# Hybrid trunk with two mixture-of-experts layers: six fixed experts instead of four, five groups of four instead of four, and the shared expert's matmuls and the sort behind the routing stage

## The reference

```python
def _moe_ffn(h, w_router, router_bias, w_gate, w_up, w_down, sh_gate, sh_up, sh_down):
    scores = jax.nn.sigmoid(jnp.einsum('bld,de->ble', h, w_router).astype(f32))
    biased = scores + router_bias.astype(f32)
    # 8 groups of 8 experts; the 4 best groups by the sum of their two best; then the best 8 experts
    ...
    w = SCALE * w / jnp.sum(w, axis=-1, keepdims=True)
    # per token: sum over its 8 experts of gate * (silu(h @ w_gate) * (h @ w_up)) @ w_down
    routed = ...
    shared = (silu(h @ sh_gate) * (h @ sh_up)) @ sh_down
    return routed + shared
```

## Time and profile before

| what | us |
|---|---|
| median of 3 runs | 1682.98 (1682.36 to 1685.25) |
| the profiled execution's time | 1685.91 |
| its span, first to last instruction | 1684.1 |
| TensorE busy in the span | 1516.5 (90%), mean granted clock 0.939 |
| experts' block of layer 0, first `gate_up` to last `gate_up` start | 461.80 to 937.61 |

### The profile page before, as it was taken

How to read it: one execution, slowest core, us unless ns; L and a number is a source line. 1 busy time by engine, 2 the same in 40 slices (tenths; PEclk the granted TensorE clock), 3 DMA queues, 4 the chain that set the end, 5 groups by cost and what they waited for, 6 DMA issues and landing times. The chain is left out here.

```text
span 1684.1 us, 25401 instructions
## 1 busy us (share of the span) xinstructions
PE 1516.5 (90%) x9626; PEld 945.3 (56%) x9626; DVE 712.2 (42%) x1610; ACT 367.8 (22%) x765; POOL 249.8 (15%) x324
## 2 busy tenths in 40 slices
PE   8999988899799989979989867989999799799795
PEld 6788668787545435535534455865555345345344
DVE  3879657432434334424433347042343234234323
ACT  3766453210311111101111120131111111011112
POOL 5789336000000000000000000001000000000000
PEclk9999999699899989989999968999999899899898
DMA  7679270022999999999999290395999999999960
GB/s 265 216 169 264 101 200 3 1 90 72 422 376 424 420 425 424 423 421 423 425 419 425 85 365 3 117 375 233 397 424 423 424 422 424 423 420 425 422 280 25
DMA packets 100774, 509.36 MB, mean 302 GB/s; under 512 B 37012, under 2 KB 42196, under 8 KB 65836
## 3 DMA queue, kind: packets, MB, share of 16 engines
q1 hardware_dynamic: 90540, 478.67, 71.4%
q0 software_dynamic: 10112, 29.05, 4.5%
HBM read 506.82 MB, written 17.10 MB: 311 GB/s over the span
## 5 line engine op out<-in xcount | busy, mean ns | idle before, releaser
L1684 PE MATMUL banks<-experts,e_xgT 128*64 128x512 f32 (+1 forms) x1408 | 313.8, 628 | 36.3 <-issue 36.2
L1684 PEld LDWEIGHTS banks<-experts,e_xgT 128*64 128x64 f32 (+1 forms) x1408 | 107.3, 137 | 211.4 <-issue 211.4
L1697 PE MATMUL banks<-x_sg,e_ys 128*128 128x272 f32 (+1 forms) x896 | 209.0, 386 | 2.7 <-ACT e_ys L1776 1.7
L1820 DVE TENSOR_TENSOR e_ac<-e_sl,banks 128x256 f32<-128x256 f32 x56 | 23.6, 421 | 440.0 <-ACT e_sl L1766 440.0
L1805 DVE TENSOR_TENSOR acc<-acc,banks 128x272 f32<-128x272 f32 (+1 forms) x448 | 189.5, 430 | 11.5 <-PE banks L1697 6.3
L268 PE MATMUL banks<-hT,dense_ring 128*128 128x272 f32 x768 | 186.0, 401 | 8.0 <-DMA dense_ring<-in_w_in 8.0
L1295 POOL DMA_INDIRECT x_xg<-rows_dram,x_idx x56 | 55.6, 993 | 874.6 <-DVE x_idx L1287 838.4
L1697 PEld LDWEIGHTS banks<-x_sg,e_ys 128*128 128x128 f32 x896 | 165.9, 190 | 30.7 <-ACT e_ys L1776 3.4
L268 PEld LDWEIGHTS banks<-hT,dense_ring 128*128 128x128 f32 x768 | 148.2, 194 | 42.4 <-issue 11.7
L1684 PE MATMUL banks<-dense_ring,e_xgT 128*64 128x512 f32 (+1 forms) x320 | 150.7, 626 | 16.0 <-issue 16.0
L1719 PE MATMUL banks<-experts,e_aT 128*64 128x512 f32 (+1 forms) x704 | 153.3, 596 | 2.5 <-DVE acc L1805 2.5
(11 more groups left out here) (421 smaller groups left out, 1947.2 us busy)
## 6 DMA issues: line engine op xcount, KB each, us to landing
experts<-in_moe_gate_up SPq DMA_DIRECT2D x88, 2048.0 KB, 26.7
experts<-in_moe_down SPq DMA_DIRECT2D x88, 1024.0 KB, 26.5
dense_ring<-in_moe_gate_up SPq DMA_DIRECT2D x20, 2048.0 KB, 26.1
e_gate_up<-in_moe_gate_up SPq DMA_DIRECT2D x20, 2048.0 KB, 30.7
dense_ring<-in_moe_down SPq DMA_DIRECT2D x40, 1024.0 KB, 26.5
dense_ring<-in_w_in SPq DMA_DIRECT2D x48, 512.0 KB, 4.8
dense_ring<-in_w_out SPq DMA_DIRECT2D x4, 2048.0 KB, 7.7
dense_ring<-in_s_w_out SPq DMA_DIRECT2D x4, 2048.0 KB, 12.0
```

The lines of the kernel that those rows point to most:

```text
L1684: mm = pe.matmul(gub[e * n:(e + 1) * n, :], xgT[:, i % 2, c, e * n:(e + 1) * n], gate_up_weights(mem, j)[:, c, :], start=(c == 0), stop=(c ...
L1697: pe.matmul(cb[m % 4][:, 0:W], ys[:, m * P:(m + 1) * P], sg[:, i % 4, :], start=True, stop=True).then_inc(cmm, 1)
L1820: dve.tensor_tensor(ac[:], sl[:], gub[:, FF:], ALU.mult).then_inc(mul, 1)
```

## The change

- `FIXED` goes from 4 to 6, and three units (`FIXED_UNITS`) of fixed experts are known before the sort.
- `WIDTHS` becomes three pairs, four times a four and four pairs, and a four and three pairs: 27 units, five of them fours. The 20 smallest experts (16 before) have 32 slots.
- Expert 5 (both halves, slot 5) is loaded behind the shared expert's weights in the routing block, in both layers; its buffer is allocated with `experts`. The gate/up half of expert 4 is loaded in the experts' block, when all four shared halves are computed; its down half, as before, behind `shared_down`. SyncE does not wait for the order until `gate_up(0)` is done.
- The routing block ends with the spread of units 0 and 1, their indices and gathers. `shared_half(0)` now follows all row transposes. Half 1, the spread of keys, in layer 0 half 2, then `turn(0)` and the sort's matmuls stand at the head of TensorE's part of the experts' block; the remaining halves (3 in layer 0; 2 and 3 in layer 1) follow `turn_act(0)`. SiLU, gating and the sort's VectorE steps move there too.
- All normalised chunks now come after the sigmoid on ScalarE (`EARLY_NORM` is gone). `xg` is no longer cleared; the copied rows use `xg` and a part of `acc`, and several small tiles use `acc` and `gsb`.

```diff
-FIXED = 4
+FIXED = 6
+FIXED_UNITS = 3
 AHEAD = 3
-EARLY_NORM = 2
...
-WIDTHS = (2, 2) + 3 * (4, 2, 2, 2, 2, 2, 2) + (4, 2, 2, 2, 2)
+WIDTHS = (2, 2, 2) + 4 * (4, 2, 2, 2, 2) + (4, 2, 2, 2)
...
 def gates_in(act, ex, i, banks, W):
     if i >= 2:
-        act.wait_ge(ex["scatter_ready"], i - 1)
+        act.wait_ge(ex["index_summed"], i - 1)
...
 def place_unit(dve, mem, ex, i, banks, W):
+    dve.wait_ge(ex["scatter_ready"], i + 1)
     if i > 0:
         dve.wait_ge(ex["index_ready"], i)
-    dve.scalar_tensor_tensor(out=ex["hit"][:], in0=banks[0][:, 0:W], scalar=mine, in1=mem["tok"][:, 0:W],
+    dve.scalar_tensor_tensor(out=ex["gsb"][:, i % 2], in0=banks[0][:, 0:W], scalar=mine, in1=mem["tok"][:, 0:W],
...
+def shared_banks(mem):
+    return [mem["bank"][b] for b in (6, 7, 6, 7)]
+
+def shared_half(pe, mem, ex, layer, j):
+    q, m = divmod(j, FC)
+    first = first_token(layer)
+    W, w_gu = T - first, shared_weights(mem)[0]
+    if j == 0:
+        pe.wait_ge(mem["shared_gate_up_ready"], 32 * (layer + 1))
+    elif j >= FC:
+        pe.wait_ge(ex["sh_silu"], m + 1)
+    for c in range(DC):
+        mm = pe.matmul(shared_banks(mem)[j][:, 0:W], w_gu[:, c, q * FF + m * P:q * FF + (m + 1) * P],
+                       mem["hT"][:, c, first:], start=(c == 0), stop=(c == DC - 1))
+    mm.then_inc(ex["sh_gate_up"], 1)
...
@@ norm_and_route, @block.sync
                 load_shared(sp, k, mem, layer)
-                if layer == 0:
-                    load_first_experts(sp, k, mem, 0)
+                load_first_experts(sp, k, mem, layer, range(4) if layer == 0 else ())
+                load_gate_up(sp, k, mem, layer, RING - 1, RING - 1)
+                load_down(sp, k, mem, layer, RING - 1, RING - 1)
...
@@ norm_and_route, @block.gpsimd
-                pool.memset(ex["xg"][:], 0.0).then_inc(ex["xg_zero"], 1)
...
@@ norm_and_route, @block.tensor
-                for i in range(min(4, 2 * NT)):
+                for i in range(2 * NT):
                     turn_rows(i)
-                shared_half(0)
-                for i in range(4, 2 * NT):
-                    turn_rows(i)
+                shared_half(pe, mem, ex, layer, 0)
...
-                shared_half(1, range(0, 3))
                 pe.wait_ge(placed, 2)
                 pe.wait_ge(rows_c, 2 * NT)
                 for i in range(2):
                     spread_unit(pe, mem, ex, i, spread_ps[i], W)
-                shared_half(1, range(3, DC))
-                shared_half(2)
-                pe.wait_ge(keyed, 1)
-                pe.matmul(key_ps[0:E, 0:E], ones[0:E, 0:E], keys[:], start=True, stop=True).then_inc(spread, 1)
-                shared_half(3)
-                pe.wait_ge(placed_by, 2)
-                pe.matmul(sort_ps[:, 2 * E:2 * E + 1], twice, rank[:], start=True, stop=True)
...
@@ experts, @block.sync
-                for j in range(FIXED, RING):
-                    load_gate_up(sp, k, mem, layer, expert(j), j)
-                load_down(sp, k, mem, layer, expert(RING - 1), RING - 1)
                 for i, stream in enumerate(UNITS):
                     after = [j + RING for j in stream if j + RING < E]
                     if after:
                         sp.wait_ge(gu, i + 1)
+                        if i == 0:
+                            sp.wait_ge(ordered, 2)
                         for j in after:
                             load_gate_up(sp, k, mem, layer, expert(j), j)
+                        if i == 0:
+                            sp.wait_ge(sh_gu, 2 * FC)
+                            load_gate_up(sp, k, mem, layer, 4, 4)
                         sp.wait_ge(dn, i + 1)
                         for j in after:
                             load_down(sp, k, mem, layer, expert(j), j)
-                    if i == 0:
-                        sp.wait_ge(sh_dn, DC)
-                        load_down(sp, k, mem, layer, expert(FIXED), FIXED)
+                        if i == 0:
+                            sp.wait_ge(sh_dn, DC)
+                            load_down(sp, k, mem, layer, 4, 4)
...
@@ experts, @block.tensor
+                shared_half(pe, mem, ex, layer, 1)
+                spread_keys()
+                if layer == 0:
+                    shared_half(pe, mem, ex, layer, 2)
                 turn(0)
+                sort_experts()
+                pe.wait_ge(adjusted, 1)
                 broadcast(2)
                 for i in range(len(UNITS)):
                     gate_up(i)
                     if i + 1 < len(UNITS):
                         turn(i + 1)
+                    if i == 0:
+                        pe.wait_ge(ordered, 2)
                     turn_act(i)
+                    if i == 0:
+                        for j in range(2 if layer else 3, 2 * FC):
+                            shared_half(pe, mem, ex, layer, j)
                     if i == 1:
                         shared_down()
...
@@ experts, @block.scalar
+                for m in range(FC):
+                    act.wait_ge(sh_gu, m + 1)
+                    act.activation(shared[:, m, 0:W], shared_banks(mem)[m][:, 0:W], ACT.Silu).then_inc(sh_act, 1)
                 turned_in(0)
```

More of the change, by code:

```diff
@@ L1233, in expert_exchange @@
     sb = lambda name, shape, dt=F32: held.enter_context(nc.sbuf_tensor(f"x{layer}_{name}", shape, dt))
[L1234 to L1237, removed]
+    ex = {"xg": sb("xg", [P, 2, D]), "selw": sb("selw", [P, AHEAD, P]), "gsb": sb("gsb", [P, 2, W]),
+          "sg": sb("sg", [P, 4, W]), "idf": sb("idf", [P, 1]), "idx": sb("idx", [P, 4, 1], I32), "cm": sb("cm", [E, 1])}
+    for name in ("going", "unit_selected", "rows_broadcast", "gates_in", "scatter_ready", "index_summed",
+                 "index_ready", "sh_gate_up", "sh_silu"):
         ex[name] = sem(name)
     ex["gathered"] = [sem("gathered_even"), sem("gathered_odd")]
+    free = mem["acc"][:].rearrange("p c t -> p (c t)")
+    ex["squares"] = mem["acc"][:, :, 0:W]
+    ex["last_rows"], ex["maskT"] = free[:, 0:D], free[0:E, D:D + W]
+    ex["keys"], ex["above"], ex["at_rank"] = (free[0:E, D + T + i * E:D + T + (i + 1) * E] for i in range(3))
     return ex
@@ L1326, in norm_and_route @@
         t8, ws = sb("t8", [P, NT, 8]), sb("ws", [P, NT])
[L1327 to L1335, removed]
+        maskT, cm = ex["maskT"], ex["cm"]
+        loaded = mem["router_loaded"]
         meaned, centred, squared, sq_summed, sd_ready, rooted, scaled, out = (sem(n) for n in (
@@ L1472, in _ @@
                 act.activation(lgT[:], lgT[:], ACT.Sigmoid, bias=bias[:, 0:1]).then_inc(scored, 1)
-                for c in range(EARLY_NORM, DC):
+                for c in range(DC):
                     normal(c)
@@ L1487, in _ @@
                     gates_in(act, ex, i, spread_ps[i], W)
-                for m in range(FC):
-                    act.wait_ge(sh_gu, m + 1)
-                    act.activation(shared[:, m, 0:W], sh_ps[m][:, 0:W], ACT.Silu).then_inc(sh_act, 1)
             @block.vector
@@ L1591, in _ @@
-                link(dve.tensor_tensor(row[:], sort_ps[0:1, E:2 * E], extras[0:1], ALU.add))
-                link(dve.tensor_reduce(rank2[0:1], row[:], AX_X, ALU.max))
-                dve.tensor_copy(mem["count"][:], rank2[0:1]).then_inc(maxed, 1)
 def experts(nc, k, mem, layer, ex):
@@ L1600, in experts @@
     shift, xg, sg = mem["unit_shift"], ex["xg"], ex["sg"]
+    maskT, cm, keys, above, at_rank = (ex[n] for n in ("maskT", "cm", "keys", "above", "at_rank"))
+    sh_gu, sh_act, shared = ex["sh_gate_up"], ex["sh_silu"], mem["shared_act"]
     gate_in, idf_ok, gathered = ex["gates_in"], ex["index_summed"], ex["gathered"]
@@ L1610, in experts @@
         cb = bank[6:] + [y0b, y1b]
-        mem["gate_up_5"] = sb("gate_up_5", [P, GATE_UP])
+        key, rank, extra = (sb(n, [E, 1]) for n in ("key", "rank", "extra"))
+        row, rank2 = sb("row", [1, E]), sb("rank2", [P, 1])
+        sort, key_ps = mem["sort_par"], atb
+        key_off, number, ranks, twice, extras = (sort[:, a:b] for a, b in (
+            (0, 1), (1, 2), (2, 2 + E), (2 + E, 2 + E + P), (2 + E + P, 2 + 2 * E + P)))
+        step, keyed, spread, placed_by, adjusted, sorted_, ordered = (sem(n) for n in (
+            "sort_step", "keys_ready", "keys_spread", "ranks_ready", "places_adjusted", "sorted", "ordered"))
+        sh_mul = sem("sh_gated")
         xgT = sb("xgT", [P, 2, DC, P])
@@ L1824, in _ @@
                         select(i + AHEAD)
+                    if i == 0:
+                        for m in range(FC):
+                            gate(m)
                     if i == 1:
```

125 lines of the change are left out of this document (54 added, 71 removed).

## The result

| | before | after |
|---|---|---|
| median of 20 runs each, us | 1682.34 (1675.95 to 1689.53) | 1692.33 (1685.56 to 1698.61) |
| the profiled execution's time | 1685.91 | 1692.55 |
| its span | 1684.1 | 1689.6 |

The ratio is 1.0055, 95% interval [1.004, 1.007]: the change costs 9.3 us (6.7 to 11.8); the medians lie 10.0 apart, as the ratio is not their quotient. The forecast was 1691.1. The runs of one kernel scatter by more than 10 us, so the ratio carries the verdict, and the spans of two single profiles only locate it.

A forecast was written before the change was run, and what follows sets the result against it. Weight transfers were taken to pace the middle of the experts' stage. Later restarts of +6.4 and +3.1 us, less 1.4 for the tails, gave +8.1: 1682.98 to 1691.1 us; forecast 1688 to 1695 (chance 0.58), range 1681 to 1699.

The forecast's parts named there:

- What bounds the stage: Middle of the experts' stage: weight transfers at 424 GB/s set the pace; a unit less on TensorE only lengthens its waits.
- When the block starts: Experts' block, now begun after GpSimd's second gather: 1.1 us earlier in layer 0, 8 us earlier in layer 1.
- Clock: TensorE at the head of the experts' block: idle beforehand lowers its clock, losing 3.0 us in layer 0, 2.2 in layer 1.
- Restart: SyncE issues expert 4's down half after the last shared_down, then all later experts: 6.4 us later in layer 0, 3.1 in layer 1.
- The hidden part: Early expert loads finish before SyncE's queue resumes behind shared_down; transfers stand still for 4 and 6 us just before.
- Tail: Behind the last four: one unit fewer saves 0.6 to 0.7 us in each layer, 1.4 us for both.
- Sum: Whole kernel: 6.4 + 3.1 - 1.4 = +8.1 us, taking the median from 1682.98 to 1691.1 us.
- 1 (the transfers get the credit): Expert 5's load in layer 1's idle time counts in full, -7.4 us, and -1.4 for the tails: 1674 us; chance 0.10.
- 2 (TensorE): TensorE bounds the experts' stage, so a unit fewer per layer saves 2 by 16.2 us: 1650 us; chance 0.03.
- 3 (no clock loss): TensorE's idle before the experts' block costs no clock, or the block starts earlier: -5.2 us, giving 1686 us; chance 0.17.
- 4 (the gather late behind expert 5): Layer 1's row stores are slowed by expert 5's load, delaying the gather: up to +5 us, giving 1696 us; chance 0.12.
- 5: An expert in a four gets more than its 32 tokens, so extra rounds run; no chance given.

The follow-up runs named there:

- before_widths: The kernel before with only the change's 27 units (five fours) in place of 28: 1680.72 us, ratio 0.9979 to the kernel before.
- after_28units: The changed kernel with 28 units (four fours) as before the change: 1691.52 us, ratio 1.0036 to the kernel before.
- before_reorder: The kernel before with SyncE's wait for shared_down and expert 4's down load moved behind the gate/up loads of experts 8 and 9: 1678.21 us, ratio 0.9969.
- after_fill: The changed kernel with shared halves 1 to 3 and both SiLUs moved back into the routing block behind the spread: 1688.06 us, ratio 1.0007 to the kernel before.
- after_busy: The changed kernel plus dummy matmuls behind the spread (50 in layer 0, 16 in layer 1), which overran the gap: 1702.45 us, ratio 1.012 to the kernel before.
- after_late5: The changed kernel with expert 5's loads issued at the head of the experts' block, not in the routing block: 1688.44 us, ratio 1.0042 to the kernel before.
- after_reorder: The changed kernel with SyncE's wait for shared_down and expert 4's down load behind the gate/up loads of 8 and 9: 1687.42 us, ratio 1.0026 to the kernel before.
- before_both: The kernel before with the change's 27 units and SyncE's shared_down wait behind the gate/up loads of 8 and 9: 1675.62 us, ratio 0.996.

## Why the prediction was right

*What bounds the stage.* Right: 424 GB/s in the middle, waits that grow by what is saved, and an end that follows the restart one to one.

*When the block starts.* Layer 0: forecast 42.5 us after the start of routing, measured 447.86 - 405.4 = 42.5. The gather went out 0.4 us earlier (+39.4), as estimated, but that is within what it does by itself: +39.4 to +39.8 in the four kernels with the order of before's blocks, +39.1 to +39.9 in the eight others. Layer 1: forecast +31.5, measured +35.0. The start follows the second gather by 0.7 us as forecast; the gather itself was 2.9 us later than before. That is no part of the change: it went out between +28.8 and +32.1 in kernels of both kinds (before +29.0, before_widths +32.1, after_28units +29.0). In the profile of after the clock is at 0.50 from 1118.8 to 1125.6, where the stage's sums of squares stand. All twelve profiles fit this: before_widths and before_reorder have such a stretch at the stage's start and gathers at +32.1 and +31.8; after_fill and after_busy have one of 3 to 4 us within the first 6 and gathers at +30.5; the seven others have none there and gathers at +28.8 to +29.1. Why the stretch falls there in some executions stays open. Of these seven, after_late5, after_reorder and after_28units start the block at +31.9 to +32.1, within 0.6 us of the forecast:

```profile
1147.86 6.61 PE L1323 MATMUL banks<-hT,dense_ring 128*128 128x256 f32 x16 [5.13 <-PEq L134]
...
1156.93 7.09 PE L1642 MATMUL banks<-experts,e_xgT 128*64 128x512 f32 x32
```

This is after_late5, with the routing's start at 1116.0.

*Clock.* Forecast 3.0 and 2.2 us. Measured against after_busy, 2.6 and 1.5 in the profile after, and 1.6 to 2.9 and 2.8 to 2.9 in the three kernels beside it. The mechanism is right and the sizes are in place, but the way to them was not: what is lost is half of the time that TensorE works until the clock is back, 447.86 to 453.2 and 1153.36 to 1156.3 in the profile after, and not a sum that grows with the idle time. The same 5.1 us of idle in layer 1 cost 1.5 us there and 2.9 in after_late5.

*Restart.* Layer 0: forecast +6.4, measured +5.4. Layer 1: forecast +3.1, measured +5.1. The gather was 2.9 us late, but the block's head then lost 1.4 us less to the clock than in after_late5, so that the restart is 1.5 to 1.6 later than in the three kernels with an early gather (+75.8 to +75.9). Those are 3.4 to 3.6 behind the early ones of before's order (+72.3 and +72.5). The mean over the four profiles with the change's order and no dummies in layer 1's gap (after, after_reorder, after_late5, after_28units) is +87.0 and +76.2, over the four with the order of before's blocks (before, before_reorder, before_widths, before_both) +81.5 and +73.1: 5.5 and 3.1 apart. The hidden part was right too: the set is in before the restart, as the holes of 184 GB/s at 490 and of 129 at 1190 show. Forecast were 4 and 6 us without transfers; against 424 GB/s the windows 488 to 498 (308) and 1188 to 1198 (172) miss 2.7 and 5.9 us. The hole at 460 to 470 I did not name as such; it lies ahead of the restart and costs nothing in the change's own order.

*Tail.* Forecast -1.4, measured -1.6 by restart to last `gate_up`, in the profile after as in the means.

*Sum.* Forecast +8.1; 5.4 + 5.1 - 1.6 = 8.9 in the profile after, 9.4 with what lies behind the last `gate_up`, 9.3 in the runs. By the means over the profiles it would be 7.0, inside the interval's 6.7 to 11.8. After's own gather was among the late ones, and I can't say how often that is so over its 20 runs. That the single profile comes within 1.3 us of the forecast is in part luck: layer 0 came 1.0 below it and layer 1 2.0 above.

*Rivals.* 1 (the transfers get the credit) fell with after_late5. 2 (TensorE) fell with before_widths. 3 (no clock loss) fell with after_busy. 4 (the gather late behind expert 5) fell:

```profile
1150.33 1.06 POOL L1300 DMA_INDIRECT x_xg<-rows_dram,x_idx  x1 [8.38 <-DVE x_idx L1292]
```

the first gather of layer 1 waited 8.38 us for its index, not for the stores. Rows 9 take in the gathers, which read `rows_dram`, beside the stores that write it; the stores alone took 2.9 to 3.0 us in layer 1 before, 4.6 to 5.0 after, and 3.0 to 3.2 in after_late5, which has no expert 5 beside them. So expert 5 did slow them, by less than 2 us, and nothing waited for them. 5 did not appear.

## What to carry to other kernels

When transfers pace a stage, look for the one moment from which they run without a break, and ask of each edit only whether it moves that moment; a prefetch that is in before it is worth nothing, however idle the transfers are. Work moved out of a gap in which an engine waits can be paid for twice, by its own time and by the clock at which it then runs. A single profile of such a stage can mislead by 3 us, so lay the places of several kernels side by side. In a queue that is issued in order, the cheapest gain may be to let a load pass a wait that isn't its own: three moved lines gave 0.3% (0.1 to 0.55), when the whole change cost 0.55%.

## What the hardware showed that I had not expected

- A longer idle gap did not cost more clock. After 13.09 us of idle TensorE worked 5.3 us at 0.50; after 1.70 and 4.20 us of it with 0.3 us of work between (after_fill, clock at 0.50 from 461.2 to 471.5, work from 463.19) it worked 8.3 us at 0.50, and lost 4.1 us instead of 2.6.
- The third row store of layer 0, of 64 KB, went out 3.8 us earlier against the start of routing than before (+23.7 and +27.5) and let the gather go only 0.4 us earlier: it took 15.8 us at most to land where it took 12.4 (issue to gather). Beside it the loads move 424 GB/s; that they set its landing is likely and was not tested.
- The two stores ahead of it, of 512 KB each, took 11.2 and 15.4 us before. The Trainium skill (DMA: Bandwidth & Descriptors, Queues, rings and completion order) has the engines take turns between queues packet by packet. By that, with packets of one size in both queues, a 512 KB store would take an estimated 2.5 us of transfer (512 KB at half of 424 GB/s); this case does not agree under full load, and in layer 1, with only expert 5 beside them, such stores landed in 4.6 to 5.0 us.
